# A two-layer transformer block on one core: the instruction order of the mixer rewritten

## The reference

```python
h += 0.5 * rms(swiglu(rms(h)))            # ffn1, hidden 2816
h += rms(mixing(rms(h)))                  # four mixers of 256 columns, w_out
h += rms(cross_attention(rms(h), rms(mem)))   # w_q, w_kv (1024 x 2048), w_o
h += 0.5 * rms(swiglu(rms(h)))            # ffn2
```

## Time and profile before

| | us |
|---|---|
| median of 3 runs (lowest, highest) | 1329.68 (1329.30, 1329.98) |
| the profiled execution | 1331.46 |
| its span | 1329.7 |
| PE busy in the span | 1284.1 (97%) |
| DVE busy | 845.5 (64%) |
| ACT busy | 683.3 (51%) |
| mean granted clock | 0.983 |

### The profile page before, as it was taken

How to read it: one execution, slowest core, us unless ns; L and a number is a source line. 1 busy time by engine, 2 the same in 40 slices (tenths; PEclk the granted TensorE clock), 3 DMA queues, 4 the chain that set the end, 5 groups by cost and what they waited for, 6 DMA issues and landing times.

```text
span 1329.7 us, 18613 instructions
## 1 busy us (share of the span) xinstructions
PE 1284.1 (97%) x6836; PEld 1096.8 (82%) x6836; DVE 845.5 (64%) x1173; ACT 683.3 (51%) x1113; POOL 235.8 (18%) x250
## 2 busy tenths in 40 slices
PE   7999999988999999999999999999899999999998
PEld 5887888778998978888878878887789888788886
DVE  5657857675666665555576577666766665755554
ACT  6455446474455554444464544554655454644443
POOL 1628900000002010000045296000000020100000
PEclk9999999998999999999999999999889999999999
DMA  9654543324334246555455555534143343555551
GB/s 345 247 189 158 204 175 127 142 96 159 127 127 167 102 170 247 189 189 189 158 181 188 188 185 189 190 112 158 64 159 127 128 171 112 215 188 189 189 189 64
DMA packets 32442, 222.65 MB, mean 167 GB/s; under 512 B 3584, under 2 KB 4096, under 8 KB 6784
## 3 DMA queue, kind: packets, MB, share of 16 engines
q1 hardware_dynamic: 30080, 209.28, 43.9%
q10 hardware_dynamic: 2304, 12.58, 2.5%
HBM read 219.75 MB, written 2.10 MB: 167 GB/s over the span
## 4 chain that ended last, share of the span: by engine, by line
PE 83%; DVE 7%; ACT 4%; issue 3%; DMA 1%; SPq 0%; POOL 0%; DVEq 0%; ACTq 0%; POOLq 0%
PE PS L1675 80%; DVE w_lo L1141 3%; PE PS L1790 1%; ACT w_hi L666 1%; DMA raw<-in_weights 1%; DVE x_lo L1144 1%; PE PS L2002 1%; ACT work L960 1%; DVE work L1144 0%; DVE work L1141 0%; DVE PS L1141 0%; DVE rope_t L1312 0%; ACT x_hi L714 0%; DVE h L1144 0%; DVE zone L1141 0%
## 5 line engine op out<-in xcount | busy, mean ns | idle before, releaser
L1141 DVE TENSOR_TENSOR w_lo<-raw,w_hi 128x1024 fp32r<-128x1024 f32 (+1 forms) x394 | 503.1, 1320 | 231.9 <-ACT w_hi L666 228.9
L666 ACT ACTIVATE w_hi<-raw 128x1024 fp32r<-128x1024 f32 x384 | 384.7, 1053 | 241.4 <-PE PS L1675 239.2
L1675 PE MATMUL PS<-w_hi,x_hi 128*128 128x512 f32 (+2 forms) x1104 | 426.9, 387 | 10.6 <-DVE x_lo L1144 5.3
L1675 PE MATMUL PS<-w_lo,x_hi 128*128 128x512 f32 (+2 forms) x1104 | 415.8, 377 | 0.0
L1675 PE MATMUL PS<-w_hi,x_lo 128*128 128x512 f32 (+2 forms) x1104 | 410.4, 378 | 0.0
L1675 PEld LDWEIGHTS PS<-w_hi,x_hi 128*128 128x128 f32 x1104 | 210.5, 191 | 53.2 <-DVE w_lo L1141 7.8
L1675 PEld LDWEIGHTS PS<-w_hi,x_lo 128*128 128x128 f32 x1104 | 210.0, 190 | 38.4
L1675 PEld LDWEIGHTS PS<-w_lo,x_hi 128*128 128x128 f32 x1104 | 211.0, 191 | 35.2 <-issue 0.5
L1675 PE MATMUL PS<-w_hi,hid_hi 128*128 128x512 f32 (+1 forms) x368 | 141.2, 386 | 0.0
L1675 PE MATMUL PS<-w_lo,hid_hi 128*128 128x512 f32 (+1 forms) x368 | 140.4, 385 | 0.0
L516 POOL TENSOR_SCALAR st<-st 128x1 f32<-128x1 f32 x32 | 20.3, 634 | 631.7 <-ACT proj L689 562.3
(11 more groups left out here) (275 smaller groups left out, 1342.1 us busy)
## 6 DMA issues: line engine op xcount, KB each, us to landing
raw<-in_weights SPq DMA_DIRECT2D x194, 1024.0 KB, 4.7
pmat<-in_mats ACTq DMA_DIRECT2D x3, 1664.0 KB, 8.0
gain<-in_post ACTq DMA_DIRECT2D x8, 512.0 KB, 3.7
zone<-mem_scratch ACTq DMA_DIRECT2D x2, 1024.0 KB, 5.8
raw<-in_weights SPq DMA_DIRECT2D x3, 512.0 KB, 7.6
h<-in_x SPq DMA_DIRECT2D x2, 512.0 KB, 6.3
zone<-in_mem SPq DMA_DIRECT2D x1, 1024.0 KB, 11.0
mem_scratch<-zone ACTq DMA_DIRECT2D x1, 1024.0 KB, 8.4
```

The lines of the kernel that those rows point to most:

```text
L666: a.activation(w_hi[s][:, c_], raw[s][:, c_], ACT.Copy).then_inc(sem[hi_done[s]], 1)
L1141: return v.tensor_tensor(o, x_, y_, op)
L1675: return t_.matmul(o, a_, b_, start=first, stop=last)
```

## The change

Only the order of the instructions and some places in memory change; the number of matmuls does not. Per layer:

- `group_half(2,1,0)` goes ahead of the latent transposes; the VectorE step `variance` for them goes ahead of the second scan.
- `group_half(3,1,1)` and the first half of key/value unit 0 go behind `scores(0)`, the S5 gate matmul behind that half. ScalarE splits the memory rows in two halves, each as soon as its `w_in` unit is done.
- The rotation (`nsa_rope`) and the transposes of the NSA queries go from before attention 0 to behind the FoX preparation.
- Key/value and `phi` units alternate in another order (`PHI_UNITS`), and from unit 1 on every key/value unit uses bank 1.
- The last attention, the compressed scores and their values go between parts of `w_out` (`out_rows(q, t, js)`, new).

```diff
-M_PHI = N_IN + 2
-KV_UNITS = [N_IN, N_IN + 1, *range(M_PHI + 4, M_PHI + 10)]
-KV_BANK = [1, 1, 1, 3, 0, 1, 0, 1]
+PHI_UNITS = [N_IN + i for i in (3, 5, 8, 10)]
+KV_UNITS = [N_IN + i for i in (0, 1, 2, 4, 6, 7, 9, 11)]
+KV_BANK = [0] + 7 * [1]
...
@@ ScalarE
-                split_mid(9)
-
...
+                act.wait_ge(*E.at("mem_in", 16))
+                for half in range(2):
+                    s, n, _ = mid(l, N_IN - 2 + half)
+                    act.wait_ge(*E.at(unit_done[s], n + 1))
+                    mem_hi(range(half * KT // 2, (half + 1) * KT // 2))
                 evac(3, 1)
...
+                split_mid(9)
                 act.wait_ge(*E.at("s5_z", 1))
...
+                attention(0)
+
+                act.wait_ge(*E.at("fox_x", 1))
+                a.activation(f_b2, f_a, ACT.Exp).then_inc(sem["fox_e"], 1)
+                act.wait_ge(*E.at("fox_e", 1))
+                a.activation(f_a, f_b2, ACT.Ln, bias=1.0).then_inc(sem["fox_ln"], 1)
                 split_mid(10)
...
@@ VectorE
-                mem_lo(range(2))
+                mem_lo(range(KT))
                 attention_max(0)
-                mem_lo(range(2, KT))
                 split_mid(9)
...
@@ TensorE
+                group_half(2, 1, 0)
+
                 pe.wait_ge(s_con, 16)
                 pe.wait_ge(*E.at("mla_xn", 1))
...
-                group(2, 1)
+                group_half(2, 1, 1)
...
-                group(3, 1)
+                group_half(3, 1, 0)
...
+                scores(0)
+                group_half(3, 1, 1)
+                pe.wait_ge(*E.at("proj_done", 8))
                 kv_half(0, 0)
...
+                def out_rows(q, t, js):
+
+                    s, _, ns = mid(l, M_OUT + q)
+                    pe.wait_ge(*E.at(split_done[s], ns + 1))
+                    pe.wait_ge(*E.at("x_split", FILL[FI_MO] + 2 * q + 2))
...
+                out_rows(1, 0, range(2))
                 pe.wait_ge(s_con, 16)
                 pe.wait_ge(*E.at("cmp_x", 1))
-                probs_transposed(1)
...
+                probs_transposed(2)
+                out_rows(0, 1, range(2))
+                times_values(2)
...
+                out_rows(2, 0, range(2))
+                out_rows(2, 1, [0])
...
+                pe.wait_ge(*E.at("grp_xn", 2))
+                mixer_transposed(MO_ORDER[6:8])
+                out_rows(2, 1, [1])
```

More of the change, by code:

```diff
@@ L1012, in _ @@
                                  ACT.Tanh, scale=GELU_S).then_inc(sem["phi_th"], 1)
[L1013 to L1016, removed]
+                evac_kv(7)
+                split_mid(22)
                 act.wait_ge(*E.at("phi_out", 1))
@@ L1523, in _ @@
                 attention_copy(3)
-                s, n, _ = mid(l, M_PHI + 3)
+                split_mid(16)
+                attention_out(3)
+                split_mid(17)
+                attention_max(1)
+                split_mid(18)
+                attention_copy(1)
+                split_mid(19)
+                s, n, _ = mid(l, PHI_UNITS[3])
                 dve.wait_ge(*E.at(unit_done[s], n + 1))
                 v.tensor_copy(phi_rows[0:2 * NC_CMP], bank(0)[0:2 * NC_CMP]).then_inc(sem["phi_h"], 1)
-                split_mid(16)
+                dve.wait_ge(*E.at("grp_sq", 1))
+                variance([(grp(ss, 0, 3, 2), 256)])
+                split_mid(20)
+                group_norm(0, 0, 3, 2)
+                dve.wait_ge(*E.at("x_hi_done", FILL[FI_MO] + 2))
+                for k in range(2):
+                    tt(s5_tiles[1][:, k], s_out[:, k], s5_tiles[0][:, k].bitcast(F32), ALU.subtract).then_inc(sem["x_split"], 1)
+                split_mid(21)
+                attention_out(1)
                 dve.wait_ge(*E.at("phi_t", 1))
@@ L2061, in kv_half, with fox_heads @@
                         i.then_inc(sem[unit_done[s]], 1)
-                pe.wait_ge(*E.at("proj_done", 9))
-                kv_half(0, 0)
+                def fox_heads(at, b, name):
+                    for hh in range(H):
+                        for t in range(TT):
+                            i = t_.transpose(v3(bank(b, 2), "p (h s) -> p h s", h=H)[0:HD, hh, t * P:(t + 1) * P],
+                                             pr3[:, t, at + hh * HD:at + (hh + 1) * HD], ident)
+                    i.then_inc(sem[name], 1)
@@ L2148, in _ @@
                 i.then_inc(sem["phi_t"], 1)
[L2149 removed]
+                kv_half(7, 1)
+                pe.wait_ge(*E.at("att_out", 3))
+                scores(2)
                 pe.wait_ge(*E.at("phi_hid", 1))
@@ L2342, in pack, with kv, phi @@
             put(u[:, KT // 2:].reshape(P, UNIT))
-        for q in range(2):
+        def kv(q):
             put(tall(g["xa_w_kv"][l][:, q * UC:(q + 1) * UC]))
-        for j in range(2):
-            for half in range(2):
-                put(tall(g["nsa_phi_w1"][l, j][half * KT * P:(half + 1) * KT * P]))
-        for q in range(2, 8):
-            put(tall(g["xa_w_kv"][l][:, q * UC:(q + 1) * UC]))
+        def phi(q):
+            put(tall(g["nsa_phi_w1"][l, q // 2][q % 2 * KT * P:(q % 2 + 1) * KT * P]))
+        for m in range(N_IN, M_OUT):
+            if m in KV_UNITS:
+                kv(KV_UNITS.index(m))
+            else:
+                phi(PHI_UNITS.index(m))
         for q in (3, 0, 2, 1):
```

362 lines of the change are left out of this document (168 added, 194 removed).

## The result

| | kernel before | changed kernel |
|---|---|---|
| time, median | 1329.83 us (4 runs, 1329.30 to 1330.63) | 1297.88 us (4 runs, 1297.24 to 1299.67) |
| ratio | | 0.9761, 95% interval 0.9744 to 0.9778 |
| profiled execution: time, span | 1331.46, 1329.7 | 1299.67, 1297.9 |
| TensorE busy | 1284.1 | 1267.9 |
| span less TensorE busy | 45.6 | 30.0 |

The change saves 31.95 us. The instructions of TensorE are the same in number (6836), so its busy time can only shrink by the clock: 1284.1 - 1267.9 = 16.2 us of clock, and 45.6 - 30.0 = 15.6 us of idle time. That is 31.8 of the 38.1 us that both mixers had to give.

The account below looks back on a forecast made before the run. Bound: TensorE's idle and low-clock time in the mixers, 19.05 us a layer, 38.1 in all. 19.05 - 4.15 (new waits) - 5.1 (clock left) = 9.8, both layers 19.6: 1311.9 profiled, 1310 us median; own range 1304 to 1316, eight in ten 1299 to 1322.

Parts of the forecast that it names:

- The latent input: Latent transposes, first layer part: a half unit ahead of them removes TensorE's wait of 2.33 us, with 0.4 to spare.
- the memory rows: Key/value half behind the first scores: the wait for memory rows in `x_lo` falls from 3.0 us to 0.3.
- attention 0: Steps of attention 0: an earlier maximum and unit halves between its steps remove both waits, 1.7 us.
- the FoX scores: At the FoX scores: the 3.0 us wait for unit 12's split goes; the delay goes to the exponentials, 1.25 us.
- The wait at the probabilities of attention 3: TensorE waits there 1.25 us a layer for ScalarE's late exponentials; the moved query rotation makes it.
- The last quarter of the output projection: End of `w_out`: four late transposes and a VectorE split ahead of the low parts make a wait of 0.75 us.
- the one bank: Rival, chance 0.05: TensorE waits for ScalarE's copies to key/value units seven times, 18 us a layer; 1354 us.
- The small waits: New TensorE waits across the mixer, 0.3 + 1.25 + 0.45 + 0.4 + 0.3 + 0.75 + 0.7 = 4.15 us a layer.
- The four terms of 0.3, 0.45, 0.4 and 0.3: Waits in us: memory rows, values of attention 3, attention 1's output for `scores(2)`, low parts of `w_out`'s second quarter.
- the tail of the post norm: ScalarE reaches the squares of the post norm 0.9 us later behind a closer split: 0.7 us.
- Clock left: Low-clock stretches left at the list's new weak places: bounds 0 and 6, 3 taken at 1.7 us = 5.1 a layer.
- the clock stays up: Rival, chance 0.15: dense half units between nearly all narrow steps leave one low stretch a layer; 26.4 us saved, 1303.

Follow-up runs that it names:

- The nine profiles: Profiles of the changed kernel or of a variant that keeps its two narrow places (all but the last run); no single time.
- the second part alone: Kernel before with only first scores between halves of unit (3,1), S5 matmul and ScalarE/VectorE lists for memory rows as changed: 1330.80 us, ratio 1.002.
- the fastest version: Changed kernel with VectorE's query rotation behind the maximum of attention 3 and the last output unit's split one place earlier: 1294.71 us, ratio 0.9744.

## Why the prediction fell short

**What was right.** The walk through the lists. The latent input, the memory rows, attention 0 and the FoX scores lost their waits. The wait at the probabilities of attention 3 was forecast at 1.25 us and is 1.3, and its cause, the query rotation, is confirmed by taking it away. The last quarter of the output projection was put at 0.75 and waits 0.9 in layer 0. The table load ahead of the exponentials cost nothing (it ends at 319.19, the maximum at 320.49). None of the copies of key/value units is waited for, so the one bank did not show.

**The small waits.** I took 4.15 us a layer; TensorE's idle time there is 2.3. The four terms of 0.3, 0.45, 0.4 and 0.3 did not come at all, and the tail of the post norm (0.7) shows no wait either. Each was a difference of a few tenths in a walk over 20 us. Both layers: 3.7 us too many, with layer 0's figure taken twice.

**The step that failed: "Clock left".** I took three low stretches a layer at 1.7 us, 5.1, halfway between 0 and six. The profile of the changed kernel has one in two layers, 0.85 a layer, and the means of its four runs (clock loss 0 to 4 us, 2 on average, the whole kernel taken) allow no more than that. That is 8.5 us in both layers. With the 3.7 it makes up the 12.2 by which the profiled executions beat the sum (31.8 less 19.6).

The cause is in how I chose three: in effect each weak place that I listed got a whole stretch, in every layer. The nine profiles tell place by place what came, of 18 layers:

- the wait of 1.25: none, behind 14 such waits;
- the values of attention 0, the S5 sum and the FoX sums "in a row (5 us of narrow matmuls, behind no wait)": 5. The place was right, the weight was not;
- `cmp_s` and `cmp_o` between projection pieces: none;
- the values of attention 1 with the 30-row matmuls, which I had not listed: 7.

That is 0.7 stretches a layer and not 3. What I held against the rival "the clock stays up" was the one stretch of the kernel before that had no wait ahead of it. It had 15-row matmuls right behind the scores, and it went when they were moved between dense pieces, which is where the change puts them. The other four stretches of each layer stood at waits that the change took away. The rival's 1303 came nearest, but it too left one stretch a layer and all the small waits, and is 5 us high.

**Where the time went.** Idle time 15.6 us and clock 16.2. By parts: the latent input is 8.6 us when undone and 6.1 (3.9 to 9.7) alone; the second part alone is nothing. The rest was not taken apart further: the runs show the parts to depend on each other, so their shares do not add up.

**What stays open.** Why the latent input's wait of 2.3 us brought a stretch in six layers of ten and not in the others, why the 15-row stretch went on for 5.8 us into dense work, and what makes the stretches at the two narrow places come in some executions and not in others.

## What to carry to other kernels

In this kernel a wait of TensorE of 3 us or more always had a low stretch with it, one of 2.3 us in about half of the cases, and one of 1.3 us or less never, but for one place with narrow matmuls behind it. So price the first at its length and about 2 us (1.4 and 2.3 for the two of the earlier trace rows), the second at its length and about 1, the third at its length. Do not count work over few rows of the array as dense work: 8.8 us of it cost 6.2 us of clock beside itself. Price a run of narrow matmuls by how often profiles show a stretch there, not as a stretch each time. When waits are removed, let the forecast of the clock fall with them rather than halfway. And a wait that is removed alone, in a chain where the next input is as late, gives nothing: test the edits together, and undo them one by one.

## What the runs showed of the chip

- The same kernel runs at different mean clocks. The kernel before had 0.983 (spans 1327.3 to 1330.2) in many executions and 0.991 (1323.0 to 1323.8) in others. The clock loss differs by 10.6 us, the time by 5.5. It would fit that slower matmuls ahead of a wait only fill the wait, but no execution at 0.991 was profiled, so this is not shown. In the fastest version, which hardly waits in the mixers, the loss comes through in full: 0.994 against 0.998 to 0.999 is 6 us of loss, 1298.5 against 1292.1 to 1293.9 of span.
- The clock fell in the middle of busy work over 15 rows (288.92 and 937.46), while the same number of 64-column matmuls over 128 rows at the same place kept it up in both layers of their profile.
